# A hybrid pool and DeltaNet layer on one core: shift and scale formed as columns in the prologue, the gate's third of w_ada moved into the first block

## The reference

```
mod = silu(c) @ w_ada + b_ada            # (1 + 8 rows) x 3072
shift, scale, gate = split(mod, 3)
h = rms_norm(x, pre_norm_w) * (1 + scale) + shift
proj = h @ w_in                          # pooling, gates, q/k/v, beta, decay
... windowed pooling; causal conv, gated DeltaNet in chunks; SiLU gates ...
x = x + gate * rms_norm(y @ w_out, post_norm_w)
```

## Time and profile before

| | |
|---|---|
| median of 3 runs | 1324.25 us (1321.76 to 1325.36) |
| the profiled execution's own time | 1325.41 us |
| its span | 1323.6 us |
| TensorE busy, matmul | 1196.2 us, 90% |
| weight loads | 967.7 us, 73% (they lie under the matmuls) |
| DVE, ACT, POOL busy | 618.0, 360.1 and 219.5 us |
| DMA | 199.26 MB, mean 151 GB/s |
| mean granted TensorE clock | 0.945 of full speed |

### The profile page before, as it was taken

One profiled execution on the slowest core, in us unless ns is written; L12 is line 12 of the kernel. 1 busy time (PEld: TensorE's weight loads), 2 busy tenths in 40 slices (PEclk: granted clock), 3 DMA queues, 4 the chain that ended last, 5 costly groups with the idle time before them and its releaser, 6 DMA issues. The chain is left out here.

```text
span 1323.6 us, 17521 instructions
## 1 busy us (share of the span) xinstructions
PE 1196.2 (90%) x6636; PEld 967.7 (73%) x6636; DVE 618.0 (47%) x1212; ACT 360.1 (27%) x690; POOL 219.5 (17%) x225
## 2 busy tenths in 40 slices
PE   5889967989899999988999999989997989999893
PEld 1258865877687878877878788768776879887672
DVE  1256562544535663445255744443435452444524
ACT  2315432223443420223324301133153220111101
POOL 0043133434320010320000103210000001321000
PEclk9988978999999999999999999999988887999897
DMA  8366146333476443223665432135732331221234
GB/s 338 156 240 252 29 146 247 136 136 116 176 286 225 179 149 125 70 94 122 228 222 191 148 131 96 64 113 209 281 117 88 104 111 42 88 91 69 112 146 149
DMA packets 69382, 199.26 MB, mean 151 GB/s; under 512 B 34578, under 2 KB 35858, under 8 KB 52020
## 3 DMA queue, kind: packets, MB, share of 16 engines
q1 hardware_dynamic: 69300, 198.15, 41.8%
HBM read 151.78 MB, written 46.35 MB: 150 GB/s over the span
## 5 line engine op out<-in xcount | busy, mean ns | idle before, releaser
L1811 PE MATMUL acc<-hhi,wsl 128*128 128x512 f32 x768 | 326.5, 425 | 0.8 <-DVE gpw L1067 0.8
L1813 PE MATMUL acc<-hhi,wsl 128*128 128x512 f32 x768 | 307.9, 401 | 0.0
L1812 PE MATMUL acc<-hlo,wsl 128*128 128x512 f32 x768 | 307.9, 401 | 0.0
L1813 PEld LDWEIGHTS acc<-hhi,wsl 128*128 128x128 f32 x768 | 149.1, 194 | 33.9
L1811 PEld LDWEIGHTS acc<-hhi,wsl 128*128 128x128 f32 x768 | 150.4, 196 | 30.8 <-DVE gpw L1067 2.4
L1812 PEld LDWEIGHTS acc<-hlo,wsl 128*128 128x128 f32 x768 | 150.4, 196 | 26.8 <-issue 1.0
L1080 DVE SCALAR_TENSOR_TENSOR cacc<-raw,cw,cacc 128x512 f32<-128x512 f32 x144 | 120.6, 838 | 5.1
L1630 POOL TENSOR_TENSOR wsl<-wraw,wsl 128x512 fp32r<-128x512 f32 x64 | 87.6, 1385 | 192.3 <-ACT wsl L819 192.3
L1077 DVE TENSOR_SCALAR cacc<-raw,cw 128x512 f32<-128x512 f32 x48 | 23.4, 487 | 156.8 <-ACT cq L872 143.8
L835 ACT ACTIVATE raw<-acc 128x512 f32<-128x512 f32 x48 | 28.7, 598 | 247.8 <-PE acc L1813 243.0
L1851 PEld LDWEIGHTS ring<-xv,lt 128*128 128x128 f32 (+1 forms) x384 | 43.0, 177 | 26.2 <-issue 13.5
(11 more groups left out here) (294 smaller groups left out, 1924.1 us busy)
## 6 DMA issues: line engine op xcount, KB each, us to landing
wsl<-kept_w SPq DMA_DIRECT2D x96, 1024.0 KB, 4.8
kept_w<-wsl SPq DMA_DIRECT2D x32, 1024.0 KB, 5.6
wraw<-in_w SPq DMA_DIRECT2D x64, 256.0 KB, 3.4
wada<-in_w_ada SPq DMA_DIRECT2D x6, 2048.0 KB, 16.2
xb<-in_x SPq DMA_DIRECT2D x16, 512.0 KB, 5.8
xres<-in_x SPq DMA_DIRECT2D x16, 512.0 KB, 5.8
out_y<-ytok SPq DMA_DIRECT2D x16, 512.0 KB, 8.2
ssm<-in_s_ssm SPq DMA_DIRECT2D x1, 2048.0 KB, 11.1
```

Of the source, the lines that this page charges most:

```text
L1811: nc.tensor.matmul(acc[t % 2][:], w[:, 0, k], hi[:, k], start=(k == 0), stop=False)
L1812: nc.tensor.matmul(acc[t % 2][:], w[:, 0, k], lo[:, k], start=False, stop=False)
L1813: last = nc.tensor.matmul(acc[t % 2][:], w[:, 1, k], hi[:, k], start=False, stop=(k == KT - 1))
```

## The change

In the prologue, only the four sixths that hold shift and scale are formed, in the order shift 0, scale 0, shift 1, scale 1, directly as columns: `w_ada` is the stationary operand (128 x 128) and the 9 columns of `cin` move, 32 products per sixth, with each sixth loaded in two halves of columns. `mod`, `amul` and `h` are made in two halves of four feature tiles; ACT makes `htmp` alone and DVE rounds it to `hhi`. The gate's two sixths are loaded in quarters in SP's loop (t = 0 to 7) and formed after tiles 3 and 7 of block 0, spread after tiles 5 and 9, in ring banks of their own (`ada`, `grow`), which other blocks leave out. The sample rows of the gate go through DRAM. `bada` and `mod` shrink to 16 columns.

```diff
+FIRST_JOBS = ("ada", "grow")
+ADA_AT = {3: 0, 7: 1}
+GROW_AT = {5: 0, 9: 1}
+def absent(kind, it):
+    return (kind in FIRST_JOBS and it != 0) or (kind == "xf" if it == NB - 1 else kind in SAMPLE_JOBS)
...
             jobs.append(("sg", 0))
+        jobs += [("ada", ADA_AT[t])] if t in ADA_AT else []
+        jobs += [("grow", GROW_AT[t])] if t in GROW_AT else []
         jobs += [("gb", c) for c in GB_AT.get(t, ())]
...
-    jobs += [("sgt", 0), ("sgt", 1)]
...
+            sp.dma_start(cin[:], a["c_all"]).then_inc(s_cin, 16)
+            modulation(0)
+            modulation(1)
...
+            modulation(2)
             sp.dma_start(xrow, a["xs"]).then_inc(sm_x0, 16)
...
             for n in range(WR):
                 raw_half(n)
+            modulation(3)
...
+            def gate_quarter(n):
+                j, e = divmod(n, 4)
+                cols = slice(e * P, (e + 1) * P)
+                sp.dma_start(wada[4 + j][:, :, cols], a["w_ada"][4 + j][:, :, cols]).then_inc(gate_in[j], 16)
...
                         split_tile(t)
+                        if t < 8:
+                            gate_quarter(t)
...
+            def first_h(m):
+                act.wait_ge(*job["xf"](PROLOGUE, m))
+                if m >= 2:
+                    act.wait_ge(*h_lo(PROLOGUE, m - 2))
+                nc.scalar.activation(htmp[:, m % 2], bank("xf", m)[:], ACT.Identity, bias=mod[:, m, 0:1],
+                                     scale=amul[:, m, 0:1]).then_inc(s_htmp, 1)
...
+                for m in range(4 * hf, 4 * hf + 4):
+                    dve.wait_ge(s_htmp, m + 1)
+                    nc.vector.tensor_copy(hhi[:, m], htmp[:, m % 2]).then_inc(h_hi.sem, 1)
+                    front_lo(dve, PROLOGUE, m)
...
+            def gate_row(m):
+                cols = slice(m * BT, (m + 1) * BT)
+                dve.wait_ge(s_gate, m + 1)
+                nc.vector.tensor_tensor(grow[:, cols], grow[:, cols], bank("ada", m)[0:1 + NS, :], ALU.add).then_inc(s_trc, 1)
+                dve.wait_ge(s_trc, 2 * m + 1)
+                nc.vector.tensor_tensor(grow[:, cols], grow[:, cols], pwr[:, cols], ALU.mult).then_inc(s_trc, 1)
...
+            def modulate(j, e):
+                pe.wait_ge(ada_in[j][e], 16)
+                for i in range(2 * e, 2 * e + 2):
+                    for k in range(KT):
+                        last = nc.tensor.matmul(spare[j // 2][:, 36 * (j % 2) + 9 * i:36 * (j % 2) + 9 * i + 9], wada[j][:, k, i * P:(i + 1) * P],
+                                                cin[:, k, :], start=(k == 0), stop=(k == KT - 1))
...
+            for j in range(3):
+                modulate(j, 0)
+                modulate(j, 1)
+            for m in range(3):
+                front_pe(pe, PROLOGUE, m)
+            modulate(3, 0)
+            front_pe(pe, PROLOGUE, 3)
+            modulate(3, 1)
+            for m in range(4, 7):
+                front_pe(pe, PROLOGUE, m)
...
+            def gate_rows_of(j):
+                pe.wait_ge(gate_in[j], 64)
+                bank_free(pe, 0, "ada", j)
...
+            def first_tile():
+                for k in range(4):
+                    tile(0, 0, k)
+                front_pe(pe, PROLOGUE, 7)
+                for k in range(4, KT):
+                    tile(0, 0, k)
+                pe.wait_ge(*done("dve", "xn"))
...
+                pe.wait_ge(s_pre, 4)
```

More of the change, by code:

```diff
@@ L573, in layer_kernel @@
                          "son": lambda n: done("dve", "ms0"), "spl": lambda n: done("dve", "yma"),
-                         "sgt": lambda n: done("dve", f"gr{n}"), "sop": lambda n: done("dve", f"sn{n}")}
+                         "sop": lambda n: done("dve", f"sn{n}")}
+        first_reader = {"ada": lambda n: (s_trc, 2 * n + 1), "grow": lambda n: (s_rowc, n + 1)}
         def bank_free(eng, it, kind, n=0, *needs):
             before, late = JOB_AT[kind, n], False
-            last = it is LAST
+            of = it
             while True:
@@ L582, in bank_free @@
                 if before < 0:
-                    before, late, last = len(JOBS) - 1, True, False
-                if JOB_BANK[before] == JOB_BANK[JOB_AT[kind, n]] and not absent(JOBS[before][0], last):
+                    before, late, of = len(JOBS) - 1, True, it - 1
+                if JOB_BANK[before] == JOB_BANK[JOB_AT[kind, n]] and not absent(JOBS[before][0], of):
                     break
@@ L728, in block_of @@
                         blocks_in(it)
+                    if t == 4 and not last:
+                        sp.wait_ge(*job["xf"](it, -1))
                     if 4 <= t < 8 and not last:
@@ L1025, in _ @@
+            dve.wait_ge(*done("pool", "rx"))
+            nc.vector.tensor_scalar(xrow, xrow, s8[:, 2:3], None, ALU.mult).then_inc(*step("dve", "xn"))
+            dve.wait_ge(s_prm2, 160)
+            nc.vector.tensor_copy(wgh[:], wgr[:]).then_inc(s_pre, 1)
             dve.wait_ge(s_pre, 2)
[L1026 to L1029, removed]
+            nc.vector.tensor_tensor(wgl[:], wgr[:], wgh[:].bitcast(F32), ALU.subtract).then_inc(s_pre, 1)
@@ L1341, in sample_out @@
                     nc.vector.tensor_tensor(ssm[:, r], ssm[:, r], heads(bank("sop", r)), ALU.add).then_inc(*s(f"sn{r}"))
[L1342 to L1346, removed]
-                                                pw8[:, e * 512:(e + 1) * 512], ALU.mult).then_inc(*s(f"gr{e}"))
             def block_of(it, last=False):
@@ L1385, in block_of @@
                         stat(it, t - SUMS)
+                    if it == 0 and t in ADA_AT:
+                        gate_row(ADA_AT[t])
+                    if it == 0 and t in GROW_AT:
+                        gate_copy(GROW_AT[t])
                     for c in GB_AT.get(t, ()):
@@ L1646, in u_tile @@
                 pool.wait_ge(*u_out(it, g - 2))
+                if it == 0 and g == 0:
+                    pool.wait_ge(gate_out, 16)
                 held(pool)
@@ L1786, in _, with gate_rows_spread @@
-            turn_rows(4, spare[1], 0)
-            turn_rows(5, spare[1], 36).then_inc(s_tr, 1)
-            pe.wait_ge(s_pre, 2)
-            pe.wait_ge(*done("dve", "h"))
-            for m in range(2):
+                last.then_inc(s_gate, 1)
+            def gate_rows_spread(m):
+                bank_free(pe, 0, "grow", m)
                 pe.wait_ge(s_trc, 2 * m + 2)
-                nc.tensor.matmul((spare[2], spare[0])[m][:], ones[0:1, :], grow[0:1, m * 512:(m + 1) * 512], start=True,
+                nc.tensor.matmul(bank("grow", m)[:], ones[0:1, :], grow[0:1, m * BT:(m + 1) * BT], start=True,
@@ L1953, in block_of @@
                     if last:
+                        if t == 0:
+                            pe.wait_ge(*done("dve", "hl"))
                         sample_tile(it, t)
-                    tile(it, t)
+                    if it == 0 and t == 0:
+                        first_tile()
+                    else:
+                        tile(it, t)
                     if t == GATES:
@@ L2076, in block_of @@
                         sample_state(it, m)
-                if last:
-                    sample_rows(it, "sgt", lambda e: mod[:, 16 + e, 1:1 + NS])
             for it in range(NB):
```

188 lines of the change are left out of this document (80 added, 108 removed).

## The result

The changed kernel takes 1355.57 us (median of 4 runs, 1352.69 to 1356.96) against 1324.8 for the kernel before (4 runs): ratio 1.0234, 95% interval 1.021 to 1.0258, so slower. The profiled execution took 1352.69 us, with a span of 1350.9 against 1323.6, 27.3 more. Forecast were 1350 as a median and 1351.5 for an execution like the profiled one. Of its four runs the profiled one is the fastest after the change (1352.69) and the slowest before it (1325.41), so the 27.3 us between the two profiles are less than the 30.8 between the medians.

The account below looks back on a forecast made before the run. TensorE, busy 90% of the span, was taken as the bound; -9.1 + 7.0 + 1.7 + 4.1 + 1.0 + 15.2 + 8.4 - 1.0 - 1.2 = +26.1 gave 1351.5 us, 1350 as median, range 1334 to 1361.

Parts of the forecast that it names:

- the single case: The summed main case: all terms with their bounds, 1343 to 1359 us, given 67%.
- Prologue: TensorE's chain up to tile 0's copy: 76.5 against 85.60 us, -9.1, with a sixth's products costing 13.6 instead of 7.03.
- My sign for it: In the prologue, granted clock 0.50 from 6 to 60 us; a clock of 1.00 would make the forecast wrong.
- the sample row: 1.8: Prologue: 8 small transposes (some 0.6), then DVE's hs, hh, hl ahead of the later steps, 1.8 us together.
- rival 1: Prologue, TensorE between 6 and 60 us: the clock rises, so the kernel is not slower, about 1321 us; 10%.
- Block 0: Block 0's added costs: gate rows 0 +7.0, spread 0 +1.7, gate rows 1 +4.1, SP's DMA queue +1.0.
- the second group: Gate rows 1 after block 0's tile 7: 7.0 more work, 3.6 absorbed by idle time, +4.1 with DVE's gate_copy(1).
- Banks, blocks 1 and 2: Shifted banks make kk 3 wait for DVE's lt: 5.5 idle plus 2.1 lower clock, 7.6 a block, +15.2 together.
- Block 3: Shifted banks: sp 6 waits behind sp 5, 6.3 + 2.1 = +8.4; kk 3 coincides with existing waits, 0.
- 2: Rival on the shifted banks: their waits don't bite, the release being earlier than read, about 1327 us; 5%.
- rival 3: Bank waits are partly absorbed: idle times stay, no clock is lost, following idle times shrink, about 1338.5 us; 12%.
- Rival 4: Block 0, tiles 1 to 4: the DMA queue fills and raw halves come late, +8, 1358 us; 6%.

Follow-up runs that it names:

- e4_late: The changed kernel with TensorE's waits for the sample row's DVE chain and the constants moved behind tile 1, in front of the gates: 1347.84 us.
- e3_wide: The changed kernel with each of the prologue's 256 products moving 128 columns instead of 9: 1335.27 us.
- e1: The changed kernel with banks for ada and grow given by hand, so other jobs keep their old bank numbers: 1332.77 us, ratio 1.0053.
- e2: The kernel before with four empty jobs put into the list where ada and grow stand after the change: 1345.74 us, ratio 1.0162.

## Why the prediction was right, point by point

The forecast was 1350 (1334 to 1361), slower at 85%; measured 1355.57. Direction and the main mechanisms, the clock of the prologue and the shifted banks, were right. Against the profiled execution it was 26.1 forecast and 27.3 measured, but that nearness is in good part luck: the medians are 30.8 apart, and the sum hides misses that cancel (prologue 5.2 too low, block 0 4.5 too high, block 3 about 4 too high, a drift of 5.6 left out). The upper end of the single case was also added up wrong: with every term at its upper bound it gives 1363, not 1359.

- **Prologue** (forecast -9.1 with the sample row, measured -3.9 at tile 1's copy). The clock, the step with the greatest doubt, was right: 13.7 us a sixth. My sign for it, a granted clock of 0.50, was not: the view reads 1.00, which by my own words would have spoken against the forecast, and the durations spoke for it. Tile 0 came within 0.5 us by luck. The 76.5 held 1.8 for the sample row, which stands behind tile 0's copy; without it the forecast for that copy is 74.7. The first product started 1.8 late, the transposes took the 5.9 forecast, and the tile with its eighth transposes 7.65 instead of 8.0. What was mis-sized is "the sample row: 1.8". I counted DVE's `hs` and two short followers, but from the start of the row's transposes (75.69) to tile 1 (79.69) it is 4.0 us, 3.34 of them idle, and the clock was then lower for tile 1, which I had at nothing. e4_late puts idle time and clock at 5.1 us. Why the followers weren't short is in the last section.
- **The Trainium skill's rule** ("TensorE: Matmul & The Clock Gate", Part 1: the lower clock is the default, and activity releases it). In this case a TensorE busy 20.00 of 20.00 us stayed at the lower level with 9, 36 and 64 moving columns, and left it with 128. By the rule, as I read it, each of them should have left it. Rows 5 had shown the direction, and rival 1 with its 29 us was a fair price: e3_wide has 25.4 us at tile 0.
- **Block 0** (forecast 7.0 + 1.7 + 4.1 + 1.0 = 13.8; measured 7.1 from tile 1 to tile 11, 9.3 to block 1's tile 7). The first gate rows cost 7.0, as forecast. The first spread took 1.12 us at the upper clock, and the table still goes down (3.1 to 2.6), since TensorE works 3.4 us at the lower clock from tile 1 to tile 7 where it worked 6.8 before. For the second group I had 4.1; by tile 11 it is 0.6 (2.6 to 3.2). The late raw halves aren't what set it: SP issues them at 168.03 instead of 162.96, but TensorE is busy until 177.91. Its added work there, 7.0 for the rows, 2.0 of waiting within `kk` and 1.1 for the spread, fills the 6.92 and leaves 3.3 (172.02 to 177.91 is 5.9, less the 2.6 of tile 7). I had 3.4 for another reason, so that nearness is luck. The term that I left out is a gain: with the idle time its lower clock goes too, and the earlier trace rows had put that at 2.7 us. The DMA's 1.0 doesn't show by itself.
- **Banks, blocks 1 and 2** (forecast 7.6 each; measured 8.3 and 8.5 from tile 7 to 8). Place, size (5.39 for 5.5) and releaser were right, and e1 and e2 show the cause from both sides. The lower clock cost about 2.8, just above my 1.5 to 2.7.
- **Block 3** (forecast +8.4 for `sp` 6, 0 for `kk` 3). `sp` 6 cost 7.8. But `kk` 3 gave back 3.5: its 5.39 us take the place of the 4.50 and 2.29 of the earlier trace rows, which I had called "coincides: 0". The outputs gave about 1.5, and the end 1.2, as forecast: from the last tile (30.0) to the span (27.3) it is 2.7.
- **Not forecast:** between the banks' waits blocks 1 and 2 lose 5.6 (13.7 to 19.3) and gain 0.8 (27.8 to 27.0). A part is TensorE's wait of 2.59 us for `xv` at 507.43 and the lower clock behind it; e1_ring also drifts by 5.8 between tile 8 of block 1 and tile 7 of block 2, with only 0.98 us of that wait. The trace accounts for both drifts: between these two tiles TensorE is idle for 12.0 us in the kernel before, 14.3 in the changed one and 13.0 in e1_ring, and its work at the lower clock lasts 3.4, 9.5 and 13.7 us. The added idle time and half of the added lower-clock time make 5.4 and 6.2 us, for 5.6 and 5.8. Why the clock falls more often there is open.

Of the rivals, 1 (the clock rises in the prologue) is out by the 13.7 us of a sixth. 2 and 3 (waits that don't bite, or are absorbed) fall by e1 and e2, except in block 3, where some of rival 3 is true. Rival 4 (raw halves late) doesn't show in the timeline.

## What to carry to other kernels

Where buffers are given out by position in a list, an entry that exists in one block only moves every later entry in all blocks. List each job's new predecessor before adding one, or give the new entries buffers by hand; here four empty entries cost 21 us. Turning a thin product so that the big matrix is stationary cost little by itself (7.4 us a sixth with 128 moving columns, against 7.03 as rows); what cost was the lower clock that came with 9 moving columns (13.7). Widening the moving operand with columns nobody reads was worth 20 us here. Ask of any wait that is put ahead of the first tile whether that tile needs it.

## What the runs showed that was not expected

- The granted clock reads 1.00 from the start until the clock's first recorded change, also where TensorE runs at half speed: 12 transposes in 2.80 us under 1.00 in the changed kernel, in 1.47 under 1.00 in e3_wide. In such a stretch the clock is to be read from the duration of a known operation.
- The same idle time may or may not be followed by a lower clock. In block 1 TensorE waits 2.50 us for `ao` in the kernel before and in e1_ring (windows right behind it, the kernel before first):

```profile
564.00:566.00 2.00, 1.11 (x7) 1.03 (x8) 1.25 (x3) 0.00 (x0) 0.00 (x0) 1.00 0.58 246
566.00:568.00 2.00, 2.00 (x13) 1.65 (x12) 0.93 (x2) 0.00 (x0) 0.00 (x0) 1.00 0.00 0
```

```profile
566.00:568.00 2.00, 1.13 (x6) 1.03 (x7) 1.12 (x3) 0.00 (x0) 0.00 (x0) 0.81 0.66 270
568.00:570.00 2.00, 2.00 (x6) 1.54 (x5) 1.05 (x2) 0.00 (x0) 0.00 (x0) 0.50 0.00 0
```

In the first the clock stays at 1.00, in the second it falls to 0.50 for the same work. Such steps of 1 to 2 us make up most of the drift between the waits; that they also make the spread of 8 us over e1_ring's runs is likely and not shown.

- The sample row's chain was long because two of its DVE instructions were. The changed kernel first (DVE, then POOL), the kernel before below:

```profile
77.16 1.15 DVE L1093 CAST hs<-hs 128x64 fp32r<-128x64 f32 x1
78.34 1.22 DVE L1095 TENSOR_TENSOR hs<-hs 128x64 fp32r<-128x64 f32 x1
...
75.76 3.71 POOL L1672 TENSOR_TENSOR wsl<-wraw,wsl 128x512 fp32r<-128x512 f32 x3 [11.96 <-ACT wsl L849]
```

```profile
69.95 0.20 DVE L1050 CAST hs<-hs 128x64 fp32r<-128x64 f32 x1
70.18 0.22 DVE L1052 TENSOR_TENSOR hs<-hs 128x64 fp32r<-128x64 f32 x1
...
70.41 3.46 POOL L1630 TENSOR_TENSOR wsl<-wraw,wsl 128x512 fp32r<-128x512 f32 x2 [0.97 <-ACT wsl L819]
```

The same two instructions take 1.15 and 1.22 us where they took 0.20 and 0.22. POOL's three instructions end at 77.03, 78.25 and 79.47, and DVE's end right behind them, at 77.12 (the one before these two), 78.31 and 79.56; in the kernel before POOL stood idle while they ran. All runs of the changed order have this, e3_wide too (DVE 52.88 and 54.07, POOL 52.80 and 54.02), and there the next one, with POOL idle, takes 0.23. So DVE's short instructions seem to end only with POOL's instruction of the raw weights' split; no run moves POOL's work away to test it.
